# Latent attention: a head pair's two groups of context queries placed between its groups of latent queries

## What is computed

```python
def block_attention(q, k, v, scale):
    ...
    def one_block(qi):
        s = jnp.einsum('bhqd,bhkd->bhqk', qi, k).astype(jnp.float32) * scale
        p = jax.nn.softmax(s, axis=-1).astype(v.dtype)
        return jnp.einsum('bhqk,bhkd->bhqd', p, v)
    ...

scale = (MLA_NOPE + MLA_ROPE) ** -0.5
a_lat = block_attention(qa_l, jnp.concatenate([ka_c, ka_l], axis=2), jnp.concatenate([va_c, va_l], axis=2), scale)
...
if need_ctx:
    y_ctx = combine(block_attention(qa_c, ka_c, va_c, scale), h_c, mo_c, z_c, u_ctx.dtype)
```

## Time and profile before

| | us |
|---|---|
| median of 3 runs | 4398.81 (4395.8 to 4404.44) |
| the profiled execution | 4409.71 |
| its span in the trace | 4406.0 |
| the attention loop in it, from the first transpose at 317.50 to the end of the last output at 720.34 | 402.8 |

### The profile page before, as it was taken

The page is one execution under the profiler, slowest core; times in us unless marked ns, Lnnn a source line. Parts: engine busy times, 40 slices in busy tenths (PEclk is TensorE's granted clock), DMA queues, the critical chain, the costliest instruction groups (busy, mean ns, idle before and its releaser), DMA issues. The chain is left out here.

```text
span 4406.0 us, 46543 instructions
## 1 busy us (share of the span) xinstructions
PE 4288.0 (97%) x18562; PEld 2508.3 (57%) x18562; DVE 1421.3 (32%) x3540; ACT 943.9 (21%) x1723; POOL 157.2 (4%) x221
## 2 busy tenths in 40 slices
PE   7999998999999999989999999999999999999998
PEld 3686666776556668577544565664544444444444
DVE  2236663665131255446244111112323300000002
ACT  2223332333123311154234211111111000000000
POOL 2000000000000000032010000010000000000000
PEclk8999999999999999989999999999999999999999
DMA  6210003112010111131021111122232111111111
GB/s 232 95 56 8 8 8 72 38 43 96 29 32 29 50 52 51 48 112 32 24 80 34 39 43 57 50 75 92 62 110 88 34 39 39 39 39 39 44 49 38
DMA packets 102693, 242.85 MB, mean 55 GB/s; under 512 B 15111, under 2 KB 44153, under 8 KB 100878
## 3 DMA queue, kind: packets, MB, share of 16 engines
q1 hardware_dynamic: 95440, 221.40, 15.8%
q0 software_dynamic: 5888, 13.25, 1.2%
q10 hardware_dynamic: 1152, 5.24, 0.3%
HBM read 202.79 MB, written 39.34 MB: 55 GB/s over the span
## 5 line engine op out<-in xcount | busy, mean ns | idle before, releaser
L2324 PE MATMUL lat_banks<-sbuf 128*128 128x512 f32 (+2 forms) x2112 | 817.1, 545 | 2.3 <-DVE sbuf L2788 2.3
L301 PE MATMUL mlp_prod<-sbuf 128*128 128x512 f32 x1792 | 771.2, 593 | 1.2 <-DVE sbuf L374 1.2
L2324 PEld LDWEIGHTS lat_banks<-sbuf 128*128 128x128 f32 x2112 | 394.9, 200 | 384.0 <-issue 377.6
L301 PEld LDWEIGHTS mlp_prod<-sbuf 128*128 128x128 f32 x1792 | 341.2, 190 | 430.7 <-issue 428.7
L1747 PE MATMUL gla_prod<-sbuf 128*128 128x512 f32 (+1 forms) x784 | 319.5, 563 | 0.0
L1224 PE MATMUL mls_banks<-sbuf 128*128 128x512 f32 (+1 forms) x768 | 284.2, 525 | 7.2 <-DMA sbuf<-in_l_w_in 6.7
L1747 PEld LDWEIGHTS gla_prod<-sbuf 128*128 128x128 f32 x784 | 147.4, 192 | 151.8 <-issue 144.9
L1224 PEld LDWEIGHTS mls_banks<-sbuf 128*128 128x128 f32 x768 | 144.4, 192 | 123.9 <-issue 109.1
L2545 ACT ACTIVATE sbuf<-lat_banks 128x512 f32<-128x512 f32 (+1 forms) x124 | 72.3, 583 | 630.9 <-PE lat_banks L2324 582.3
L749 PE MATMUL mla_banks<-sbuf 128*128 128x512 f32 (+1 forms) x416 | 176.0, 511 | 0.0
L350 ACT ACTIVATE sbuf<-mlp_prod 128x1024 f32<-128x1024 f32 x32 | 32.8, 1024 | 635.1 <-PE mlp_prod L301 635.1
(11 more groups left out here) (432 smaller groups left out, 5305.2 us busy)
## 6 DMA issues: line engine op xcount, KB each, us to landing
sbuf<-in_l_w_in SPq DMA_DIRECT2D x59, 512.0 KB, 3.9
sbuf<-in_w_in SPq DMA_DIRECT2D x52, 512.0 KB, 4.1
sbuf<-in_w_mlp_in SPq DMA_DIRECT2D x32, 512.0 KB, 3.6
sbuf<-in_w_mlp_out SPq DMA_DIRECT2D x32, 512.0 KB, 3.6
sbuf<-in_l_w_mod SPq DMA_DIRECT2D x12, 1024.0 KB, 13.4
sbuf<-in_l_w_mod SPq DMA_DIRECT2D x24, 512.0 KB, 5.0
scratch_gates<-sbuf SPq DMA_DIRECT2D x48, 256.0 KB, 3.0
sbuf<-scratch_gates SPq DMA_DIRECT2D x8, 1536.0 KB, 6.5
```

Source lines behind the costliest of these rows:

```text
L301: last = nc.tensor.matmul(prod[:, n % NB, o:o + 512], w[:, n % NB, k * P:(k + 1) * P], rhs, start=k == 0, stop=k == KD - 1)
L2324: last = nc.tensor.matmul(dst, lhsT, rhs, start=k == 0, stop=k == KD - 1)
```

## The change

The order of the ten query tiles of each head pair changes. Before, the eight latent tiles come first and the two context tiles behind them. After, context tile 0 stands behind three latent tiles and context tile 1 behind three more, and two latent tiles follow. All 40 groups, with their instructions, buffers and semaphores, are the same in number and kind; everything else that depends on a group's place (batches, counts, which buffer of two, three or four a group uses) is derived from the list.

```diff
-    groups = [(j, t) for j in range(4) for t in list(range(2, TT)) + [0, 1]]
+    groups = [(j, t) for j in range(4) for t in (2, 3, 4, 0, 5, 6, 7, 1, 8, 9)]
```

## The result

| | before | after |
|---|---|---|
| median | 4399.76 us (4395.8 to 4404.44, 6 runs) | 4416.95 us (4413.84 to 4420.45, 6 runs) |
| ratio | | 1.0037 (95% interval 1.0027 to 1.0046) |
| profiled execution's span | 4406.0 us | 4414.7 us |
| the attention loop in it | 402.8 us (317.50 to 720.34) | 417.9 us (314.88 to 732.74) |

A forecast was written before the change was run, and what follows sets the result against it. The attention loop was taken as bound by a ring of PE transposes and DVE/ACT copies around one bank; 4398.8 us plus 19.0 (15.6 for steps and last group, 3.3 for clock) gave 4417.8 us, range 4406 to 4428.

The forecast's parts named there:

- The prices of the steps: Attention loop's time as a sum of fixed prices by kinds of group and follower: 399.2 us before, 414.8 after.
- CL: Attention loop step of a context group followed by a latent group, priced at 7.03 us.
- LL: Attention loop step of a latent group followed by a latent group, priced at 11.11 us.
- Why the kinds differ: Next group's latent scores hide in a latent group's copy time, but cost nearly their own length in a context group's step.
- the 0.84: Extra us in the latent step behind a context group, 11.95 against 11.11, from a late maximum and DVE's output before the copy.
- The tail: Last latent group ending the loop: 10.8 us (9.5 to 11.4) against 3.79 for the last context group, adding 7.0.
- The clock in the LC steps: PE's clock falls in four of eight latent-to-context steps, 1.66 us each: 6.6 against 3.3 before, adding 3.3 us.
- LC: Attention loop step of a latent group followed by a context group: 10.69 us, or 12.35 where PE's clock falls.
- Faster: Rival: latent steps before context groups become limited by PE's work, 7.69 us each; kernel 4387 to 4390 us; chance 0.04.
- The clock spared: Rival: dense latent scores after the thin steps prevent clock falls; change costs 12.3 us, kernel 4411 us; chance 0.14.
- The clock hit everywhere: Rival: all nine thin places in the loop pay for clock falls; change costs 27.2 us, kernel 4426 us; chance 0.11.
- An even trade: Rival: late copy vanishes, last group costs 9.5 us, clock stays up; 4.3 us slower, 4403 us; chance 0.08.

The follow-up runs named there:

- ctx_end: Kernel before, with all 32 latent groups first, pair by pair, and the eight context groups behind them: 4394.79 us, ratio 0.9982.
- last_old: New order in the first three head pairs, old order in the last one: 4409.16 us, ratio 1.0016 to the kernel before.
- last_new: Old order in the first three head pairs, new order in the last one: 4410.24 us, ratio 1.0020 to the kernel before.
- few_scores: New order, with scores of the first 1024 keys left out for every latent group but the first: 4438.26 us in one run.
- copy_first: New order, but DVE makes the next latent step's first copy before the preceding context group's output: 4416.0 us, ratio 1.0030 to the kernel before.

## Why the prediction was right

The forecast was 4417.8 us, 19.0 above the kernel before; measured were 4416.95 and, by the ratio, 16 above (12 to 20), or 17 by the medians. Point by point:

- **The prices of the steps** were right, nearly every step to 0.02 us, in all orders. The exceptions come at the same places in each profile of an order: the first two steps behind a CL (11.91 and 12.32 for 11.95) and one LL step of the old order (11.34 to 11.36), with three in ctx_end. The neighbourhood L-C-L, new in this change, kept CL at 7.03. The medians' differences of last_old, last_new and ctx_end lie within 0.5 us of the prices. Part of that is luck, as their intervals are 4 us wide to each side and the falls of the clock are not in these prices.
- **Why the kinds differ** was right: few_scores shows latent scores hidden in LL and, for 1.97 of their 3.4 us, exposed in CL. The copy behind the output and the late maximum as the causes of the 0.84 were right: 0.56 and 0.28 in copy_first.
- **The tail** was put at 10.8 us within 9.5 to 11.4. With the clock up it is 11.2 (filled, so not quite the same thing); in fact it was 13.0 to 13.5 in all five profiles, above these bounds, because there the clock always fell: of the 2.66 that the first one took over 10.8, its weighing alone has 4.54 - 2.40 = 2.14, and it began 5.5 us before the end and not 3.3. The fall in the tail stood only in the upper bound of the clock, so this term was 2.2 to 2.7 us too small. Step 38, the LL without queries, was rightly left at 11.11.
- **The clock in the LC steps** was too large. From the one profile I took four falls of eight against two of four, +3.3 us; the first profile of the new order had none, which is -3.3. The counts of all profiles (7 in 48 against 5 in 13) give 8 x 0.15 x 1.66 = 1.9 against 4 x 0.38 x 1.66 = 2.6, so -0.6. If only the first LC step of a pair can pay, both orders have four such steps, and the term is nothing. So this term was 3.3 to 3.9 us too large and the tail's about 2.5 too small, and that they cancel for the greater part is luck: the total would be 15.6 + 2.5 - 0.6 = 17.5, or 18.1, rather than 19.0, next to the measured 16 to 17. That the forecast came within 1 us of the median is luck too, as the kernel before came out 0.95 above the median that the forecast started from.
- **The profiled executions** agree: by the prices, the loop of after is 414.8 + 2.7 for the tail + 0.4 for one step (below) = 417.9; measured 417.9. The forecast for it was 18.9 us more than before, and it ended at 732.74, not at 739, as no LC step fell. The rest of the kernel, outside the loop, took between 3996.8 and 4003.2 us in the five profiles of the two unchanged kernels, in no relation to the order. That is why the spans of the first two profiles differ by only 8.7 us.
- **The rivals** fell. Faster: no LC step came below 10.67. The clock spared: its 12.3 us still lie at the edge of the interval, so the time alone doesn't refute it; the falls in seven of 48 LC steps and in each last group do. The clock hit everywhere: 27.2 us are outside, and most LC steps didn't pay. An even trade: the steps behind a CL kept 11.95, and the tail was above its bound. As for the rule of the Trainium skill ("Perfetto Trace Analysis", section "Optimization Strategy"), that interleaving regimes whose most-contended engine differs may help: the time went the other way in this loop, and ctx_end, the least mixed order, is the fastest. But PE is the busiest engine in both of ctx_end's windows (67.28 of 70 us and 30.58 of 40), so this loop says little on stretches where that engine changes.

Open: why all falls were in the first LC step of a pair. The clock fell inside the LC step, before its followers began, and among these first steps alone 7 in 24 and 5 in 13 can't be told apart, so nothing shows that the followers matter. Open too is a step of 12.32 instead of 11.95 us, the one behind the second CL, in all profiles of the unchanged new order: in the first of them DVE's reciprocal there has a gap of 0.3 us before it that the profile puts down to nothing it shows.

## What to carry to other kernels

Price a pipelined loop by its steps and their neighbours, not by the engines' shares: work of a follower may be free beside one kind of step and cost more than half of its length beside another, and then each change of kind has a price. Here the order with one change from latent to context was the fastest of the five orders run and the one with eight the slowest, their loops 25 us apart (392.8 and 417.9). End such a loop with its shortest group, as nothing covered the last one. And read a term that comes and goes between executions, such as the clock, from several profiles; one that had two of four was no measure of its odds, and list the falls by place before calling them chance.

## What the runs showed of the hardware

- With PE's work cut by 3.4 us per latent group, the loop became 22 us longer (440.3 against 417.9), as PE's granted clock fell in 17 of its 40 steps, in all eight behind a CL. Less work on an engine that waits anyway can cost time.
- Eight context groups with PE at 76% over 40 us kept 1.00, while the last latent group, with PE busy for 1.53 and then 1.60 or 1.61 us of its first two 3 us and never idle for over 0.8 us at a time, fell in all five profiles, and with matmuls in its gaps in neither of two.
- The same instructions don't always fare alike: of 61 unfilled LC steps the clock fell in 12, all of them among the 37 that come first or alone in their pair.
